# A 16-step substitution on VectorE done as two of eight steps and a corner product, and a branch's output and a short convolution placed later in the loop

## The reference

```python
h = rmsnorm(x, norm_w);  p = h @ w_in              # the big matmul over all columns of w_in
# branch A: delta rule, 16 heads of 64, after a token shift
s = s * w_t - (s @ kh_t) b_t^T + v_t k_t^T;  y_t = s @ r_t      # sequential in t
oa = (groupnorm(y) + bonus) * silu(g)
# branch B: SSD with a width-4 causal convolution, per-group rmsnorm
xbc = silu(causal_dwconv(xbc, conv_w) + conv_b);  y = ssd_chunked(xs * dt, dt * a, bm, cm) + d_skip * xs
ob = rmsnorm_group(y * silu(z))
# branch C: short convolution of width 3
oc = bg * causal_dwconv(cg * xin, conv_w) * silu(g)
merged = sum over the three of sigmoid(gate) * (branch @ w_branch)
out = rmsnorm(x + merged @ w_out, final_norm_w)
```

## Time and profile before

| | before |
|---|---|
| median of 3 runs | 1229.02 us |
| the profiled execution | 1225.43 us |
| span of its trace | 1223.7 us |
| TensorE busy | 1174.0 us, 96% |
| VectorE busy | 813.5 us, 66% |
| ScalarE busy | 577.9 us, 47% |
| mean granted TensorE clock | 0.993 |

### The profile page before, as it was taken

How to read it: one execution, slowest core, us unless ns; L and a number is a source line. 1 busy time by engine, 2 the same in 40 slices (tenths; PEclk the granted TensorE clock), 3 DMA queues, 4 the chain that set the end, 5 groups by cost and what they waited for, 6 DMA issues and landing times.

```text
span 1223.7 us, 23692 instructions
## 1 busy us (share of the span) xinstructions
PE 1174.0 (96%) x8502; PEld 1041.4 (85%) x8502; DVE 813.5 (66%) x1270; ACT 577.9 (47%) x828; POOL 69.8 (6%) x93
## 2 busy tenths in 40 slices
PE   6998899999999999999999999999999999999996
PEld 5997889899898898988989978888888888888885
DVE  4786859679587696885867956564555565546553
ACT  5454446354364463544635535544444444444443
POOL 2001001010010010100101002000000000000000
PEclk9998999999999999999999999999999999999998
DMA  5755545445455454454553546566666666668662
GB/s 165 207 155 134 157 130 141 132 114 148 129 154 150 120 141 132 136 151 126 150 133 106 145 140 184 169 206 189 191 200 194 188 191 194 196 186 274 197 194 97
DMA packets 254747, 197.24 MB, mean 161 GB/s; under 512 B 23943, under 2 KB 207472, under 8 KB 254064
## 3 DMA queue, kind: packets, MB, share of 16 engines
q1 hardware_dynamic: 252228, 195.82, 55.4%
q10 hardware_dynamic: 2476, 0.84, 0.2%
HBM read 193.71 MB, written 2.11 MB: 160 GB/s over the span
## 4 chain that ended last, share of the span: by engine, by line
PE 84%; DVE 8%; issue 3%; DMA 2%; ACT 2%; SPq 1%; DVEq 0%; POOL 0%; ACTq 0%
PE ps L1141 12%; PE ps L1219 11%; PE ps L1220 11%; PE ps L1221 11%; PE ps L1142 11%; PE ps L1143 11%; DVE wlo L716 2%; PE ps L1463 2%; PE ps L1462 2%; PE ps L1464 2%; DVE lots L879 2%; DVE lots L882 1%; ACT whi L422 1%; DVE lots L724 1%; PE ps L1253 1%
## 5 line engine op out<-in xcount | busy, mean ns | idle before, releaser
L716 DVE TENSOR_TENSOR wlo<-raw,whi 128x1024 fp32r<-128x1024 f32 (+1 forms) x356 | 440.4, 1250 | 276.6 <-ACT whi L422 276.2
L422 ACT ACTIVATE whi<-raw 128x1024 fp32r<-128x1024 f32 (+1 forms) x356 | 371.6, 1053 | 300.6 <-PE ps L1221 182.0
L1141 PE MATMUL ps<-hhi,whi 128*128 128x256 f32 (+1 forms) x1440 | 423.4, 294 | 9.0 <-DVE wlo L716 9.0
L1142 PE MATMUL ps<-hlo,whi 128*128 128x256 f32 (+1 forms) x1440 | 407.9, 283 | 0.0
L1143 PE MATMUL ps<-hhi,wlo 128*128 128x256 f32 (+1 forms) x1440 | 407.7, 283 | 0.0
L1141 PEld LDWEIGHTS ps<-hhi,whi 128*128 128x128 f32 (+1 forms) x1440 | 274.6, 191 | 25.2 <-DVE wlo L716 11.6
L1142 PEld LDWEIGHTS ps<-hlo,whi 128*128 128x128 f32 (+1 forms) x1440 | 275.2, 191 | 0.7
L1143 PEld LDWEIGHTS ps<-hhi,wlo 128*128 128x128 f32 (+1 forms) x1440 | 274.9, 191 | 0.3
L1219 PE MATMUL ps<-whi,hhi 128*128 128x512 f32 x384 | 151.4, 394 | 0.0
L1221 PE MATMUL ps<-whi,hlo 128*128 128x512 f32 x384 | 149.6, 390 | 0.0
L1220 PE MATMUL ps<-wlo,hhi 128*128 128x512 f32 x384 | 149.5, 389 | 0.0
(11 more groups left out here) (263 smaller groups left out, 1146.0 us busy)
## 6 DMA issues: line engine op xcount, KB each, us to landing
raw<-in_w_in SPq DMA_DIRECT2D x548, 256.0 KB, 3.1
raw<-in_w_branch SPq DMA_DIRECT2D x96, 256.0 KB, 3.7
raw<-in_w_out SPq DMA_DIRECT2D x64, 256.0 KB, 3.6
o<-in_x SPq DMA_DIRECT2D x4, 1024.0 KB, 6.7
acb<-acs_rows SPq DMA_DIRECT2D x8, 256.0 KB, 3.8
out_y<-lots SPq DMA_DIRECT2D x3, 512.0 KB, 4.6
lots<-in_final_norm_w SPq DMA_DIRECT2D x1, 1024.0 KB, 10.2
lots<-ad SPq DMA_DIRECT2D x32, 8.0 KB
```

The costliest lines, as they stand in the source:

```text
L422: sc.activation(whi[:, slot, :, 0:width], raw[:, slot, :, 0:width], ACT.Copy).then_inc(hi_done, 1)
L716: tt(wlo[:, slot, :, 0:width], raw[:, slot, :, 0:width], whi[:, slot, :, 0:width].bitcast(F32), ALU.subtract).then_inc(lo_done, 1)
L1141: mm(dst, a, khi, start=first, stop=False)
L1142: mm(dst, a, klo, start=False, stop=False)
```

## The change

Four things, all within the main loop (and one constant in the setup):

1. The solve. The 16x16 unit triangle is split into two diagonal blocks of 8 and the corner. Both diagonal blocks are solved at once, in 7 steps of 2 x k x k elements (`solve_step`). Then the corner is the product of three 8x8 matrices, in two products of 512 elements with a reduction to 64 each (`solve_corner`): the new array `sol_w` holds the first. VectorE does steps 1 to 4 at t = 9, 5 to 7 and the first corner product at t = 10, the second one and the copy at t = 12.
2. The delta-rule chain starts one half-chunk earlier (`V_P1` 17, `V_ST` 24). ScalarE issues its two `tb` DMAs at t = 15. On VectorE, the convolution of branch B moves from t = 13 to 19, the `seg_times` from 15 to 21, the gate of branch B from 17 to 20.
3. The output of branch B moves behind the chain: `xs2` at t = 22, its transposes at t = 25, `yb` at t = 27, into the upper half of bank E instead of bank C.
4. The short convolution moves to t = 29 and 30 on VectorE; the group norm's five operations move to t = 32, ahead of `shift_rk` (33); `kk_floor` goes from their middle to t = 35. The split of slot t = 26 comes behind that slot's state step.

Besides, `t32` gets its own array `t32p` with 32 zeroed columns ahead, and the first small matmul of uw writes 64 rows with them. The number of matmuls stays.

```diff
-V_P1 = 18
-V_XT = 20
-V_YB = V_P1 + 4
+V_P1 = 17
+V_XT = 25
+V_YB = 27
 V_ST = V_P1 + 7
...
# ScalarE
-                    if t == 17:
+                    if t == 15:
                         act.wait_ge(s["sol_tr"], j + 1)
                         for q in range(2, 4):
                             act.dma_start(tb[:, q, :, :], sol_2[8 * q:8 * q + 8, :, :, :]).then_inc(s["t_in"], 16)
-                        act.wait_ge(s["x_s"], j * 4 + 4)
-                        sc.activation(cvt, cv, ACT.Tanh, scale=0.5).then_inc(s["x_th"], 1)
...
                     if t == V_P1 + 4:
                         act.wait_ge(s["yx_mm"], j + 1)
                         sc.activation(yy, A, ACT.Copy).then_inc(s["yx_ok"], 1)
+                        act.wait_ge(s["x_s"], j * 4 + 4)
+                        sc.activation(cvt, cv, ACT.Tanh, scale=0.5).then_inc(s["x_th"], 1)
...
# VectorE
                 def solve_step(k):
-                    r = BLK - 1 - k
-                    a = slice(r + 1, BLK)
-                    prod = sol_m[:, 0:k * k].rearrange("p (t i) -> p t i", i=k)
+                    r = 7 - k
+                    prod = sol_m[:, 0:2 * k * k].rearrange("p (h t i) -> p h t i", h=2, i=k)
+                    n = sol_n8[:, :, 17 * r + 1:17 * r + 1 + k]
+                    x = sol_t8[:, :, 33 * (r + 1):33 * (r + 1) + 32 * k].rearrange("p h (i t) -> p h t i", t=32)[:, :, 0:k, :]
                     if k > 1:
-                        dve.wait_ge(s["sol_r"], j * 15 + k - 1)
-                    tt(prod, sol_n[:, r, a].unsqueeze(1).broadcast_to([32, k, k]),
-                       sol_t[:, a, a].rearrange("p i t -> p t i"), ALU.mult).then_inc(s["sol_p"], 1)
-                    dve.wait_ge(s["sol_p"], j * 15 + k)
-                    v.tensor_reduce(sol_t[:, r, a], prod, AX.X, ALU.add).then_inc(s["sol_r"], 1)
+                        dve.wait_ge(s["sol_r"], j * 9 + k - 1)
+                    tt(prod, n.unsqueeze(2).broadcast_to([32, 2, k, k]), x, ALU.mult).then_inc(s["sol_p"], 1)
+                    dve.wait_ge(s["sol_p"], j * 9 + k)
+                    v.tensor_reduce(sol_t8[:, :, 33 * r + 1:33 * r + 1 + k], prod, AX.X, ALU.add).then_inc(s["sol_r"], 1)
+
+                def solve_corner(k):
+                    a, b = slice(0, 8), slice(8, 16)
+                    prod = sol_m[:, 0:512].rearrange("p (r t i) -> p r t i", r=8, i=8)
+                    left, right, dst = ((sol_n[:, a, b], sol_t[:, b, b], sol_w[:]) if k == 8 else
+                                        (sol_t[:, a, a], sol_w[:], sol_t[:, a, b]))
+                    dve.wait_ge(s["sol_r"], j * 9 + k - 1)
+                    tt(prod, left.unsqueeze(2).broadcast_to([32, 8, 8, 8]),
+                       right.rearrange("p i t -> p t i").unsqueeze(1).broadcast_to([32, 8, 8, 8]), ALU.mult
+                       ).then_inc(s["sol_p"], 1)
+                    dve.wait_ge(s["sol_p"], j * 9 + k)
+                    v.tensor_reduce(dst, prod, AX.X, ALU.add).then_inc(s["sol_r"], 1)
...
-                    if t == 34:
+                    if t == V_ST + NC + 4:
                         dve.wait_ge(s["var_rt"], j + 1)
                         v.reciprocal(rin, nrm).then_inc(s["ln_v"], 1)
                         dve.wait_ge(s["ln_v"], j * 4 + 1)
                         tt(yo, yc, rin, ALU.mult).then_inc(s["ln_v"], 1)
-                    if t == 34 and not last:
-                        kk_floor(j + 1)
-                    if t == 34:
                         dve.wait_ge(s["ln_v"], j * 4 + 2)
...
+                    if t == 33 and not last:
+                        shift_rk(j + 1)
+                    if t == 35 and not last:
+                        kk_floor(j + 1)
...
# TensorE: `yb` out of the block at t = V_P1 + 4, into its own
+                    if t == V_YB:
+                        pe.wait_ge(s["xst_ok"], j + 1)
+                        pe.wait_ge(s["seg_g"], j + 1)
+                        for e in range(2):
+                            h = slice(64 * e, 64 * e + 64)
+                            mm(E[h, T:2 * T], xst[:, 0, h], seg[:, e, 0:T], start=True, stop=False, skip_group_check=True)
+                            op = mm(E[h, T + P:2 * T], xst[:, 1, h], seg[:, e, T:384], start=False, stop=True,
+                                    skip_group_check=True)
+                        op.then_inc(s["yb_mm"], 1)
```

More of the change, by code:

```diff
@@ L123, in build_program @@
         tx = lot(28).rearrange("p (q w n) -> p q w n", q=4, w=2)
-        p1, t32 = (lot(29)[:, n * P:n * P + P].rearrange("p (q n) -> p q n", q=4) for n in range(2))
+        p1 = lot(29)[:, 0:P].rearrange("p (q n) -> p q n", q=4)
         ys, yc, ysq = lot(28), lot(29), lot(12)
@@ L163, in build_program @@
         ad = sb("ad", [P, 4, BLK])
+        t32p = sb("t32p", [P, 5, 32])
+        t32 = t32p[:, 1:5, :]
         tb = sb("tb", [P, 4, 2, BLK])
@@ L891, in main @@
                 for t in range(2 * (LAST + GATES) if last else SLOTS):
-                    if t % 2 == 0 and t // 2 < nchunks:
+                    if t % 2 == 0 and t // 2 < nchunks and t != V_ST + 2:
                         split_lo(base + t // 2 + AHEAD, (t // 2 + AHEAD) % RING)
@@ L955, in main @@
                         op.then_inc(s["state_ok"], 1)
[L956 to L972, removed]
+                    if t == V_ST + 2 and t // 2 < nchunks:
+                        split_lo(base + t // 2 + AHEAD, (t // 2 + AHEAD) % RING)
+                    if t == 33:
                         dve.wait_ge(s["oc_hi"], j + 1)
@@ L983, in main @@
                     if t == 10:
[L984 removed]
+                        for k in range(5, 8):
                             solve_step(k)
[L986 to L988 removed]
+                        solve_corner(8)
                     if t == 12:
[L990 to L992 removed]
+                        solve_corner(9)
+                        dve.wait_ge(s["sol_r"], j * 9 + 9)
                         v.tensor_copy(sol_l, sol_t.rearrange("p s t -> p t s")).then_inc(s["sol_tr"], 1)
[L994 removed]
+                    if t == 19:
                         dve.wait_ge(tile_out, nt + 1)
                         conv4(s["x_s"], j * 4, j)
[L997 removed]
+                    if t == 21:
                         dve.wait_ge(s["dat_ok"], 1)
@@ L1009, in main @@
                         tt(bon, E[:, T:2 * T], sh[:, 2, :], ALU.mult).then_inc(s["bon_ok"], 1)
+                    if t == 20:
+                        dve.wait_ge(tile_out, nt + 2)
+                        stt(zp[:, 1, :], zp[:, 1, :], 1.0, zp[:, 0, :], ALU.add, ALU.mult).then_inc(s["z2_ok"], 1)
                     if t == V_YB + 1:
                         dve.wait_ge(s["yb_mm"], j + 1)
-                        stt(cv, xs2, dskh[:, bass.ds(j, 1)], C[:, 0:T], ALU.mult, ALU.add).then_inc(s["ob_d"], 1)
+                        stt(cv, xs2, dskh[:, bass.ds(j, 1)], E[:, T:2 * T], ALU.mult, ALU.add).then_inc(s["ob_d"], 1)
                         dve.wait_ge(s["ob_d"], j + 1)
@@ L1019, in main @@
                         stt(yc, C[:, 0:T], -1.0 / 64, ys, ALU.mult, ALU.add).then_inc(s["yc_ok"], 1)
-                    if t == 33 and not last:
-                        shift_rk(j + 1)
-                    if t == 34:
+                    if t == 29:
+                        dve.wait_ge(s["ob_ok"], j + 1)
+                        dve.wait_ge(s["sc_cx"], j + 1)
+                        for k in range(3):
+                            if k:
+                                dve.wait_ge(s["sc_s"], j * 3 + k)
+                                op = stt(scy, scx[:, k:k + T], col(SCW + k * CT), scy, ALU.mult, ALU.add)
+                            else:
+                                op = ts(scy, scx[:, 0:T], col(SCW), None, ALU.mult)
+                            op.then_inc(s["sc_s"], 1)
+                    if t == 30:
+                        stt(scc, scc, 1.0, scb[:, 3, :], ALU.add, ALU.mult)
+                        dve.wait_ge(s["sc_s"], j * 3 + 3)
+                        stt(scy, scy, 0.5, scb[:, 0, :], ALU.mult, ALU.mult).then_inc(s["sc_b"], 1)
+                        dve.wait_ge(s["sc_b"], j + 1)
+                        tt(scf, scy, scc, ALU.mult).then_inc(s["sc_f"], 1)
+                    if t == V_ST + NC + 4:
                         dve.wait_ge(s["var_rt"], j + 1)
@@ L1341, in main @@
                         pe.wait_ge(s["yx_ok"], j + 1)
-                        pe.wait_ge(s["xst_ok"], j + 1)
-                        pe.wait_ge(s["seg_g"], j + 1)
-                        for e in range(2):
-                            h = slice(64 * e, 64 * e + 64)
-                            mm(C[h, 0:T], xst[:, 0, h], seg[:, e, 0:T], start=True, stop=False, skip_group_check=True)
-                            op = mm(C[h, P:T], xst[:, 1, h], seg[:, e, T:384], start=False, stop=True,
-                                    skip_group_check=True)
-                        op.then_inc(s["yb_mm"], 1)
                         for q in range(4):
```

35 lines of the change are left out of this document (15 added, 20 removed).

## The result

Nine runs of the changed kernel took 1228.37 to 1233.41 us, median 1232.38; the kernel before, run beside it, gives the ratio 1.0028 (95% interval 1.0016 to 1.0041); one of its nine runs took 1639.19 us, a third more than the others, and is not in the ratio. So the change made the kernel slower by 0.28%, some 3.4 us, just past what a measurement can tell. The forecast was 1228.7 us, by its sum no difference, with chances of 0.38 on faster, 0.28 on the same and 0.34 on slower. The range held the time, but the sum showed no loss and the largest chance stood on the wrong side.

The account below looks back on a forecast made before the run. The loop goes at TensorE's pace, so only its waits can be won. -23.4 + 0.4 + 18.9 - 1.3 + 5.1 = -0.3 us gives 1225.1 profiled, 1228.7 as median with 3.6 us added; range 1216 to 1237.

Parts of the forecast that it names:

- Three waits of TensorE: Main loop: waits for `tx`, a late `wlo` and a state update in the last state step, together 23.4 us.
- Part 1, the solve: VectorE's triangle solve: corner products 1.13 us, reductions 0.68 us, so the solve's copy comes 1.7 us earlier.
- Part 2, the path to `tx`: From the solve's copy to `tx`: less work between; with the solve it removes 23.4 us and adds 0.4.
- A tie at V_P1: `tx` ready at 463.1, just when TensorE reaches that block; 0.05 us put on it, 0.4 in 8.
- Part 3, the new wait: Iteration's end: TensorE's block 34 waits for the square of `kk`, 2.7 us in 7 iterations, +18.9 us.
- Part 4, the clock: Clock falls to half pace after three of seven new waits, 1.7 us each, +5.1; one earlier fall dropped, -1.3.
- The distance from profile to median: Median of the runs 3.6 us above the profiled execution; kept for the changed kernel, 1225.1 to 1228.7 us.
- the slower rival: Clock falls after each of the seven new waits: +6.5 us, 1235.5 us; chance 0.20.
- Full gain: Block 34 does not wait for the group norm's chain: -24.3 us, 1204.7 us; chance 0.13.
- clock never falls: The new wait comes but the clock stays full: -5.4 us, 1223.6 us; chance 0.08.
- The late corner: Solve's corner products take 1.5 us or above, `tx` late by 0.74: +6 us, 1234.7 us; chance 0.07.

Follow-up runs that it names:

- e1: Changed kernel with the group norm moved back behind `shift_rk` and `kk_floor` in its midst: 1200.73 us, ratio 0.9789 to the kernel before.
- a run with six: The changed kernel, unchanged, run again on another chip: 1233.2 us, ratio 1.0046 to the kernel before.
- e7: Changed kernel with three group norm operations left ahead of `shift_rk` and the other two behind it: 1215.44 us, ratio 0.9907 to the kernel before.
- e5: Changed kernel with the group norm behind `shift_rk` and the old solve of 15 steps: 1217.64 us, ratio 0.993 to the kernel before.
- e2: Kernel before with only the group norm put ahead of `shift_rk` and `kk_floor` taken from its midst: 1264.85 us, ratio 1.0316.
- e3: Kernel before with the new solve alone, nothing else moved: 1208.14 us, ratio 0.985.
- e4: Changed kernel with only the group norm's reciprocal left ahead of `shift_rk`, its other four operations behind: 1208.3 us, ratio 0.9854 to the kernel before.

## Why the prediction was wrong

The place and the cause of the new wait were right; what failed is the size of two terms of the sum, the wait (+18.9, measured 22.4) and the falls of the clock (+5.1, measured 5.6 in the mildest execution and about 11 in another). Both were too small, so the sum came out even where the kernel got slower.

**What bounds it: right.** Three waits of TensorE were all that could be won, and all but 1.1 us of them went (the changed kernel's list, and e1's time).

**Part 1, the solve: right in its terms.** Corner products 1.12 and 1.10 us for 1.13, reductions 0.68 for 0.68. From start to copy it gained 2.0 us instead of 1.7.

**Part 2, the path to `tx`: right.** A tie at V_P1, 1.1 us in all what is left of the waits where 0.4 was put. The gain without the norm's wait was forecast at 1204.7, with the 3.6 us between profile and median in it; by profiled executions that is 1201.1, and e1 had 1200.56.

**Part 3, the new wait: right in place and cause, 3.5 us too small.** Here is the first mis-sized term. The prediction had 2.7 us each, +18.9. It is 3.2 each by the iterations' lengths, +22.4. Half of the 0.5 is in the chain: 9.23 us instead of 9.0, as from the reciprocal to `shift_rk` it takes 4.10 and not 3.83. The rest is that I took 0.1 us off the wait because it "counts as busy": that is right for what the list shows and wrong for the price, and TensorE's slower restart, 0.11, is missing.

**Part 4, the clock: the mechanism right, the number of falls too small.** This is the second. "I take three", +5.1. The first profile has four, at 1.4 us each and not the 1.7 that I put on one, 5.6; the second has eight stretches, about 1.4 each by the iterations' lengths, 11. The distance from profile to median was taken over from the kernel before as 3.6 us; it was 4.0, because the first profile happened to be the mildest of nine executions (granted clock 0.989, the others 0.985 to 0.987). So where the prediction added a fixed distance, it was probably adding falls, and the kernel's usual execution, 1232.38 us, is about as near to the slower rival (falls behind each wait, 1235.5) as to the forecast. That the time still fell so close to the forecast is luck in part: a fall was priced 0.3 us too high and counted too seldom, and the gain came out 0.5 larger.

The account closes on both profiles to within 0.8 us. e1, seven waits and the falls: 1200.56 + 22.4 + 4 x 1.4 = 1228.6, measured 1228.37; with 11.0 for the eight stretches 1234.0, measured 1233.34. Against the forecast of 1228.7 for the median: +3.5 for the wait, +0.5 for the clock in the first profile, +0.4 for the distance, -0.5 since the gain was larger, gives 1232.6; measured 1232.38.

**The rivals.** Full gain and "clock never falls" are out by the changed kernel's own rows. The late corner is out by 1.12 us. The slower one, seven falls and 1235.5 us, decided from five on; a run with six was measured, and the time came out on its side.

The trade was so even (23.4 against 22.4) that only its smallest terms set the sign, and of those, the falls of the clock are not a fixed number. A larger share on slower would have been right by the same rows.

## What to carry to other kernels

In a program in which every engine keeps its written order, ask of each moved block not what it waits for but what stands behind it: `shift_rk` needed nothing of the group norm, and being written behind it cost some 30 us (from e1, 0.9789 of the kernel before, to the changed kernel, 1.0028 and 1.0046 of it), more than the whole gain of 26. Move a block that waits for a long chain behind everything that another engine wants soon, and when a change has several parts, time it with each order of the last ones, since one misplaced block can hide the gain of all the rest. A new wait of TensorE is to be priced at its length in the iteration, measured from one matmul's start to another's, plus the falls of the clock behind it, and by several executions.

## What the runs showed of the hardware

- With recurring waits ahead of the same matmul, the granted clock fell more often the longer they were: to 1.2 GHz within or right behind none of seven waits of 0.73 us, one of seven of 1.86, four and six of seven of 2.90, all seven of 3.54. Up to 1.86 us the clock was next to free here; from there the falls more than doubled the price of lengthening the wait (from e7 to the changed kernel beside it the listed wait grew by 1.04 us, 7.3 in all, and the median by 17.8).
- Length alone doesn't decide it. In e5 eight waits of 1.65 to 2.79 us ahead of another matmul had no fall at all. In e2 three of the seven waits of 1.48 us ahead of L1297 had one, in the profile of the kernel before one of eight such waits. Whether the longer waits between them did that, or only where each fell in that execution, no run separates.
- A stretch of 3.4 us at 0.50 costs 1.25 to 1.6 us of time, less than the 1.7 that half pace throughout would. Both falls that came within a wait lasted 6.8 us; every fall in the loops that came behind one lasted 3.4. The ten preambles agree, with their wait of 3.6 to 4.0 us ahead of the first norm matmul: in seven the clock fell within it and stayed low for 6.8 us, in three (e1, e3, e7) it fell 0.5 to 0.8 us behind its end, for 3.4.
- A wait costs TensorE's loop 0.2 to 0.4 us more than the profile lists (e1, e3, e4, e7). For 2.90 listed it was 0.3: 0.15 from the modelled end of the matmul before, 0.11 from a slower restart.
- A product on VectorE with a strided second operand takes about 1.9 ns per further element, from 64 to 225 elements and on to 512, and 2.2 ns per element in all at 512. The product of 128x512 with contiguous operands takes 1.3 ns per element (684 ns).
